# A two-block float32 transformer on one core: PE transposes and squares in the head, the memory's transposes in step 4, and the places of some weight splits

## The reference, cut to what matters

```python
mem_n = rmsnorm(mem, mem_norm)                      # 256 x 1024, used by both layers
for l in range(2):
    x = x + 0.5 * swiglu(rmsnorm(x, g1[l]), gate, up, down)      # 1024 -> 2816 -> 1024
    x = x + mixer(rmsnorm(x, g2[l]))                # l=0: short convolution and window attention; l=1: block attention
    x = x + cross_attention(rmsnorm(x, g3[l]), mem_n, w_q, w_kv, w_o)
    x = x + 0.5 * swiglu(rmsnorm(x, g4[l]), gate, up, down)
x = rmsnorm(x, final_norm)
# second block: swiglu, convolution beside gated linear attention, swiglu, a gated projection, rmsnorm
```

## Time and profile before

| | |
|---|---|
| profiled execution, own time | 1594.08 us |
| its span, first to last instruction | 1592.4 us |
| median of three executions | 1593.88 us |
| PE busy | 98% of the span |
| DVE busy, ACT busy | 71%, 52% |
| mean granted PE clock | 0.996 |

### The profile page before, as it was taken

One profiled execution on the slowest core, in us unless ns is written; L12 is line 12 of the kernel. 1 busy time (PEld: TensorE's weight loads), 2 busy tenths in 40 slices (PEclk: granted clock), 3 DMA queues, 4 the chain that ended last, 5 costly groups with the idle time before them and its releaser, 6 DMA issues.

```text
span 1592.4 us, 23728 instructions
## 1 busy us (share of the span) xinstructions
PE 1563.0 (98%) x9061; PEld 1368.6 (86%) x9061; DVE 1126.9 (71%) x1605; ACT 829.9 (52%) x1164; POOL 80.8 (5%) x139
## 2 busy tenths in 40 slices
PE   8899999999999999999999999999999999999997
PEld 7788899898888888889988888888888998888886
DVE  6776768667666776675766776687666796776666
ACT  5554546555545555455555545455454631554444
POOL 0400002000000000000000190000000000000000
PEclk9999999999999999999999999999999999999999
DMA  8855653545655565555444655546555450456551
GB/s 279 253 176 197 185 184 133 185 133 185 209 187 174 170 212 182 194 182 163 151 133 137 223 196 174 197 150 218 205 184 180 125 185 27 141 210 210 184 187 52
DMA packets 208528, 280.62 MB, mean 176 GB/s; under 512 B 5182, under 2 KB 183784, under 8 KB 208456
## 3 DMA queue, kind: packets, MB, share of 16 engines
q1 hardware_dynamic: 206080, 274.50, 51.6%
q0 software_dynamic: 1360, 3.80, 0.8%
q10 hardware_dynamic: 1016, 1.32, 0.3%
HBM read 278.55 MB, written 2.63 MB: 177 GB/s over the span
## 4 chain that ended last, share of the span: by engine, by line
PE 89%; DVE 7%; ACT 2%; DMA 1%; issue 1%; DVEq 0%; SPq 0%; ACTq 0%
PE bank L1557 38%; PE bank L1608 29%; PE bank L1607 13%; DVE w_lo L946 3%; PE bank L1610 2%; PE bank L2037 2%; PE bank L1666 1%; ACT w_hi L522 1%; PE bank L1815 1%; PE bank L1786 1%; PE bank L1804 1%; DMA raw<-in_ffn_w_up 0%; DMA raw<-in_ffn_w_gate 0%; DMA raw<-in_xa_w_q 0%; ACT xT L550 0%
## 5 line engine op out<-in xcount | busy, mean ns | idle before, releaser
L946 DVE TENSOR_TENSOR w_lo<-raw,w_hi 128x1024 fp32r<-128x1024 f32 x514 | 617.0, 1229 | 221.2 <-ACT w_hi L522 220.4
L1608 PE MATMUL bank<-xT,w_hi 128*128 128x512 f32 x2112 | 734.9, 397 | 1.2 <-DVE w_lo L1217 1.0
L522 ACT ACTIVATE w_hi<-raw 128x1024 fp32r<-128x1024 f32 x514 | 526.4, 1051 | 148.1 <-PE bank L1608 81.7
L1607 PE MATMUL bank<-xT,w_lo 128*128 128x256 f32 x1848 | 516.3, 279 | 0.0
L1608 PEld LDWEIGHTS bank<-xT,w_hi 128*128 128x128 f32 x2112 | 383.0, 188 | 75.9 <-DVE w_lo L1217 1.4
L1607 PEld LDWEIGHTS bank<-xT,w_lo 128*128 128x128 f32 x1848 | 348.9, 189 | 12.1
L1557 PE MATMUL bank<-w_hi,hid_hi 128*128 128x512 f32 x528 | 207.6, 393 | 1.5 <-DVE w_lo L946 1.5
L1557 PE MATMUL bank<-w_hi,hid_lo 128*128 128x512 f32 x528 | 205.8, 390 | 0.0
L1557 PE MATMUL bank<-w_lo,hid_hi 128*128 128x512 f32 x528 | 205.8, 390 | 0.0
L1557 PE MATMUL bank<-xT,w_hi 128*128 128x256 f32 x800 | 146.0, 285 | 1.1 <-DVE w_lo L946 1.1
L1557 PEld LDWEIGHTS bank<-xT,w_hi 128*128 128x128 f32 x800 | 125.2, 192 | 2.5 <-DVE w_lo L946 1.5
(11 more groups left out here) (263 smaller groups left out, 1633.6 us busy)
## 6 DMA issues: line engine op xcount, KB each, us to landing
raw<-in_ffn_w_down SPq DMA_DIRECT2D x44, 1024.0 KB, 5.5
raw<-in_ffn_w_in SPq DMA_DIRECT2D x44, 1024.0 KB, 5.1
raw<-in_ffn_w_gate SPq DMA_DIRECT2D x43, 1024.0 KB, 5.3
raw<-in_ffn_w_up SPq DMA_DIRECT2D x43, 1024.0 KB, 5.4
raw<-in_ffn_w_out SPq DMA_DIRECT2D x22, 1024.0 KB, 5.3
raw<-in_w_in SPq DMA_DIRECT2D x10, 1024.0 KB, 5.3
raw<-in_xa_w_kv SPq DMA_DIRECT2D x8, 1024.0 KB, 5.8
raw<-in_od_w_in SPq DMA_DIRECT2D x8, 1024.0 KB, 5.7
```

What stands on the lines that cost most here:

```text
L522: act.activation(hi, src, ACT.Copy).then_inc(sem["hi_ready"], 1)
L946: dve.tensor_tensor(lo, src, hi.bitcast(F32), ALU.subtract).then_inc(sem["lo_ready"], 1)
L1607: pe.matmul(bank[:, b, T:2 * T], lo, xT_hi[:, k, :], start=False, stop=False)
L1608: last = pe.matmul(bank[:, b, :], hi, xT[:, k, :, :], start=k == 0, stop=k == KD - 1)
```

## The change

1. PE issues 13 transposes of the identity into bank 5 before it waits for the first gains, and 8 more between the transposes of x and the first matmul.
2. In the head ACT does `xT_his` for k 4 to 7 directly behind the splits of halves 0 and 1; the two squares of x stand later, one ahead of and one behind the late splits of halves 2 and 3. DVE's root stands behind those splits.
3. The root of the memory stands between DVE's steps 2 and 3, its scaling is now ACT's, between steps 3 and 4. PE transposes it in the step j=4: banks 0 and 1 between the two down halves (waits for `gate_summed`), banks 2 and 3 behind them (waits for `up_summed`). ACT and DVE take it out behind the hidden values of step 4.
4. At the five borders behind row projections one split stands between the first and the second residual; at the first of them another one moves into `norm`, behind the last residual.
5. In step 0 of every FFN the split base+3 stands ahead of SiLU on ACT, and between the product and `hid_lo` on DVE.

```diff
@@ ACT, ffn_step @@
                     if after_sums is not None:
                         after_sums()
+                    split(i, base + 3)
                     silu()
...
-                for n in range(5 if j == NJ - 1 else 4 if j else 3, n_splits):
+                for n in range(5 if j == NJ - 1 else 4, n_splits):
@@ ACT @@
+            def memory_scale():
+                c.next("mem_rstd_ready")
+                for t in range(NT):
+                    act.activation(mem_in[:, t, :], mem_in[:, t, :], ACT.Copy, scale=mem_rstd[:, t:t + 1])\
+                        .then_inc(sem["mem_normed"], 1)
...
                     ffn_step(f, 2)
-                    ffn_step(f, 3, after_hidden=lambda: xT_his(COL_OF["mem"], memT_hi, by_bank=True))
-                    ffn_step(f, 4)
+                    ffn_step(f, 3)
+                    memory_scale()
+                    ffn_step(f, 4, after_hidden=lambda: xT_his(COL_OF["mem"], memT_hi, by_bank=True))
@@ ACT, head @@
-            act.wait_ge(sem["x_loaded"], 16)
-            act.wait_ge(sem["x1_loaded"], 16)
-            mean_square(0)
-            mean_square(1)
             xT_his(COL_OF["ffn1"], xT_hi, ks=range(4, KD))
             act.wait_ge(sem["second_part_loaded"], 16)
             first_split(2, early, "first_hi_ready")
             first_split(3, early, "first_hi_ready")
+            act.wait_ge(sem["x_loaded"], 16)
+            act.wait_ge(sem["x1_loaded"], 16)
+            mean_square(0)
             act.wait_ge(raw_ready[1], landed[1])
             first_split(2, late, "hi_ready")
             first_split(3, late, "hi_ready")
+            mean_square(1)
@@ DVE, norm and ffn_step @@
                 residual_part(1, 1, scale)
+                splits(n_splits)
                 xT_los(gain, xT_hi, xT_lo, ks=range(4, KD))
...
-                if j == NJ - 1:
-                    split(i, base + 4)
+                if j in (0, NJ - 1):
+                    split(i, base + (4 if j else 3))
                 dve.wait_ge(sem["hidden_hi_ready"], plus(f.j0 + j + 1, 2))
@@ DVE, ffn @@
-                    memory_scale()
                     ffn_step(f, 2)
-                    ffn_step(f, 3, after_hidden=lambda: xT_los(COL_OF["mem"], memT_hi, memT_lo, by_bank=True))
-                    ffn_step(f, 4)
+                    memory_rstd()
+                    ffn_step(f, 3)
+                    ffn_step(f, 4, after_hidden=lambda: xT_los(COL_OF["mem"], memT_hi, memT_lo, by_bank=True))
@@ DVE, head @@
-            rstd_of_both()
             first_split(2, late, "hi_ready", 3, "lo_ready")
             first_split(3, late, "hi_ready", 4, "lo_ready")
+            rstd_of_both()
@@ DVE, borders: ev_w_out, xa_w_o (cross), od_w_out, w_out_2 @@
-            splits(7)
-            add_residual(1.0)
+            splits(5)
+            add_residual(1.0, between=split)
...
-                norm(COL_OF["xa"] + KD * l, scale=1.0, n_done=end, q_factor=128.0 ** -0.5)
+                norm(COL_OF["xa"] + KD * l, scale=1.0, n_done=end, q_factor=128.0 ** -0.5, n_splits=1 - l)
...
-                splits(4)
-                add_residual(1.0)
+                splits(3)
+                add_residual(1.0, between=split)
...
-            splits(8)
-            add_residual(1.0)
+            splits(7)
+            add_residual(1.0, between=split)
...
-            splits(4)
-            add_residual(1.0)
+            splits(3)
+            add_residual(1.0, between=split)
@@ PE, ffn @@
-                        if j == 4 and i is None and n in (0, 2):
+                        if j == 5 and i is None and n in (0, 2):
                             c.next("xT_lo_ready", 2)
...
-                    down(j - 1, v0 + 6 * j + 2, between=memory if j == 3 else None)
+                    if j == 4:
+                        down(j - 1, v0 + 6 * j + 2, between=lambda: memory(0), after=lambda: memory(1))
+                    else:
+                        down(j - 1, v0 + 6 * j + 2)
@@ PE @@
-            def memory():
-
-                c.next("mem_normed", 2)
-                pe.wait_ge(sem["gate_summed"], 4)
-                pe.wait_ge(sem["up_summed"], 4)
-                for k in range(KD):
+            def memory(part):
+
+                if part == 0:
+                    c.next("mem_normed", 2)
+                    pe.wait_ge(sem["gate_summed"], 5)
+                else:
+                    pe.wait_ge(sem["up_summed"], 5)
+                for k in range(4 * part, 4 * part + 4):
...
+            def keep_busy(n):
+
+                for _ in range(n):
+                    pe.transpose(bank[:, 5, 0:P], ident[:, :], ident[:, :])
+
             pe.wait_ge(sem["pool_const"], 4)
+            keep_busy(13)
             pe.wait_ge(sem["first_gains_loaded"], 32)
...
                     x_transposes(t, (k,))
+            keep_busy(8)
             ffn(loaded=True)
```

More of the change, by code:

```diff
@@ L297, in build @@
             hi_ready lo_ready half_done
-            residual mean_sq mem_normed diag_ready scale_psum scale_ready scaled xT_psum xT_hi_ready xT_lo_ready acc_ready
+            residual mean_sq mem_rstd_ready mem_normed diag_ready scale_psum scale_ready scaled xT_psum xT_hi_ready xT_lo_ready acc_ready
             gate_part_ready up_part_ready gate_summed up_summed gate_scaled up_scaled act_gate_ready hidden_ready hidden_hi_ready hidden_lo_ready
@@ L952, in splits, with rsqrt @@
                     split()
-            def rsqrt(dst, src, tmp, tmp2):
+            def rsqrt(dst, src, tmp, tmp2, done="dve_step"):
                 link(dve.tensor_scalar(src, src, EPS, None, ALU.add))
@@ L967, in rsqrt @@
                 link(dve.scalar_tensor_tensor(tmp, tmp, -0.5, src, ALU.mult, ALU.mult))
-                link(dve.scalar_tensor_tensor(dst, tmp, 1.5, dst, ALU.add, ALU.mult))
+                link(dve.scalar_tensor_tensor(dst, tmp, 1.5, dst, ALU.add, ALU.mult), done)
             def rstd_of_both():
@@ L989, in xT_los, with norm @@
                         last.then_inc(sem["xT_lo_ready"], 1)
-            def norm(gain, scale, n_done, q_factor=None):
+            def norm(gain, scale, n_done, q_factor=None, n_splits=0):
                 xT_los(gain, xT_hi, xT_lo, ks=range(4))
@@ L1109, in ffn_step @@
                 else:
-                    for n in range(4 if j else 3, n_splits):
+                    for n in range(4, n_splits):
                         split(i, base + n)
@@ L1196, in y_lo, with memory_rstd @@
                     dve.tensor_tensor(lo, src, hi.bitcast(F32), ALU.subtract).then_inc(sem["y_lo_ready"], 1)
-            def memory_scale():
+            def memory_rstd():
                 c.next("mean_sq", 2)
-                rsqrt(mem_rstd, mem_sq, small[:, 4:6], small[:, 6:8])
-                for t in range(NT):
-                    dve.tensor_scalar(mem_in[:, t, :], mem_in[:, t, :], mem_rstd[:, t:t + 1], None, ALU.mult)\
-                        .then_inc(sem["mem_normed"], 1)
+                rsqrt(mem_rstd, mem_sq, small[:, 4:6], small[:, 6:8], done="mem_rstd_ready")
             def vector_columns():
@@ L1727, in gate_up, with down @@
                         wide(v + n, n, i, between=(lambda: scale_broadcast(4)) if late and j == 1 and n == 2 else None)
-                def down(j, v, i=None, between=None):
+                def down(j, v, i=None, between=None, after=None):
                     ready = j0 + j + 1
@@ L1738, in down @@
                             between()
+                    if after is not None:
+                        after()
                 if loaded:
```

## The result

The changed kernel has a median of 1582.76 us (four executions, 1580.93 to 1585.06); the kernel before, run on the same chip beside it, 1593.11 us (four, 1592.17 to 1595.42). The ratio is 0.9932 with a 95% interval of 0.9919 to 0.9945. The forecast was 1582.7 us. The total came out; the terms that make it did not, as the rest of this document shows. The profiled execution is the longest of the four: 1585.06 us, with a span of 1583.3 us.

The account below looks back on a forecast made before the run. PE, busy for 98% of the span, was taken to bound the kernel. Memory 6.8, borders 2.9, step 0 1.0 and head 0.5 sum to 11.2 us, giving 1582.7 us; own range 1580 to 1584.5, 8 in 10 1579.5 to 1588.5.

Parts of the forecast that it names:

- the memory part: Memory transposes moved to step 4 in halves: 7.1 us of wait and low clock gone, less 0.3 us, worth 6.8 us.
- the head: Start of the kernel, idle transposes and later squares and root: gain 0.5 us, bounds 1.9 us gain to 1.5 us loss.
- the borders: Five borders behind row projections: all PE waits for residuals go, 2.9 us gained, bounds 1.8 to 2.9 us.
- I take 0.3 us: At gate_up(5), behind the memory's second half: PE's new wait would be 0.3 us, near the undisturbed step.
- the upper bound of 2.2 us: At gate_up(5): largest new PE wait, with all 2.1 us of ACT's scalings delaying a step already 1.6 us late.
- loads are issued sooner: First FFN: argument against a moved memory wait, since DVE has lost its scalings; no size of its own.
- the memory's wait moves along: Step 4's up weights reach ACT late, PE waits about 4.2 us at gate_up(5), clock falls: 1589.8 us; chance 0.13.
- PE's next half starts about 0.65 us earlier: End of the head: PE's first half of step 1 starts about 0.65 us sooner; 0.5 us taken on average.
- the forecast's branch: In the head: idle transposes hold PE's clock up; eight transposes behind half 0 take 0.9 us, not 1.63.
- the rival (0.30): In the head: idle transposes do not raise the clock, step 1 starts 1.5 us later, 1584.7 us; chance 0.30.
- The fear of a wait at the residual (1,0): At the borders: the moved remainder (about 1.2 us) delays this residual; gain only 1.8 us if some wait returns.
- Step 0 of the fifth FFN: Split ahead of SiLU lets PE start at 1071.95 instead of 1072.91: 1.0 us gained, bounds 0.5 and 1.3 us.

Follow-up runs that it names:

- the changed kernel's second profile: The changed kernel run once more with nothing changed against it: median 1582.52 us (5 executions).

## Why the prediction was right, and where it was wrong

**The total** (1582.7 forecast, 1582.76 measured) is right by luck, because errors cancel: the memory part was far too large, the head and the borders too small.

**Memory: wrong, in its first sentence.** "Gone are the 4.36 us, 3.65 - 1.75 = 1.90 us of slow transposes and 3.60 - 2.72 = 0.88 us of slow matmuls: 7.1 us" is a correct price of the wait and a wrong assignment. It was priced as if no other part touched that wait. The head's edits already take about 5.5 of the 7.1 us (2.78 us of waiting and 2.78 us of low clock), which left the wait of 1.58 us (with all the other parts 0.71 + 0.68 = 1.4 us). Then "I take 0.3 us" for the new wait failed: it was 1.74 us in one profile and 2.60 us, beyond the upper bound of 2.2 us, in the other. That step assumed that the weights of step 4 come as in an undisturbed step. Its argument "loads are issued sooner" was true (by 5.7 us), but the earlier issue left the load beside POOL's transfers for its whole way, and it landed only 1.2 us sooner. So some 1.5 us of gain and 1.7 us of new wait: nothing.

**The rival "the memory's wait moves along" (0.13)** had half of the mechanism: a late up unit and a wait at `gate_up(5)`, in the profiled execution with a fall of the clock. But the late unit is not the next one, which ACT was to split in step 4: ACT does that split at 86.24 without a wait. It is again the one that ACT got at 72.15 before (70.91 now), and its lag is carried into step 4. The rival had the size wrong (4.2 us), and it, too, counted the old wait as wholly this part's.

**Head: the start of step 1 right, the part wrong.** "PE's next half starts about 0.65 us earlier" is 0.53 to 0.78 us in the profiles. The step that failed is the one that let the head end there. For the borders the text had followed a moved remainder to "SP's load that it releases"; for the two remainders of the head, which free the first `raw` slot, it hadn't. They are what counts: through the late gate unit, 3.0 us for every later load up to the memory.

**Idle transposes: the forecast's branch was right and the rival (0.30) wrong.** Without them the first eight transposes of x take 1.97 us in all five profiled kernels that lack them, and the next eight 1.63 to 1.91 us. With them the first eight take 1.09 to 1.97 us in the nine that have them, and the next eight 1.03 or 1.04 us in every one. In seven of the nine the first eight take under 1.97 us, so the level rose before they were done, with only transposes on PE until then; in the other two it rose within the eight idle ones behind them, which take 1.23 and 1.32 us instead of 1.04. The Trainium skill says that the full clock doesn't engage for transposes (TensorE: Matmul & The Clock Gate, Part 4: PE-mode transpose); these rows contradict it. In time the idle transposes by themselves are worth 1.1 us by the medians, with no change inside the interval.

**Borders: mechanism right, term mis-sized.** All five waits are gone. The sum of 2.9 us took the idle for the cost; it is 4.0 to 4.2 us. Each wait costs about 0.2 us more than its idle, which explains 1.0 us of the difference. The fear of a wait at the residual (1,0) was unfounded.

**Step 0 of the fifth FFN: right.** Forecast 1.0 us, 1.16 us in the chain; the wait that is left was forecast at about 0.5 us and is 0.26.

**The range and the signs.** The median lies in the forecast's own range of 1580 to 1584.5 us; one result can't show how good the chances were. The granted clock was to stay at 1.00 from 20 us on; up to the last 2 us it did in the changed kernel's second profile, and not in the first, so this differs between executions of the same kernel.

## What to carry to other kernels

Price a wait once, and ask of every part of a change whether it reaches that wait: parts that shorten the same one don't add, and the fall of the clock behind it goes to whichever part brings the wait down first. Follow a moved instruction to the load that it releases and to the landing, not only the issue, of every load behind that, since a few microseconds in a prologue can come back where an in-order engine is short of weights much later; and look at what else uses the DMA when the load would now run. At these borders a wait of PE costs its idle plus about 0.2 us of draining and restarting.

## What the runs showed of the hardware

- Transposes of a 128x128 float32 identity on an otherwise unused PE raise its clock to 2.4 GHz: with thirteen idle ones ahead, the next eight take 1.09 to 1.97 us and the eight idle ones behind them 1.03 to 1.32 us (1.04 in seven of nine profiles), where the first eight without them take 1.97 us. The column of the granted clock shows nothing of this; it reads 1.00 through the head of all these kernels, and only the durations tell.
- In the first FFN, PE's clock fell to 1.2 GHz after waits of 2.13, 2.60, 3.07, 3.55, 3.63 and 4.36 us and stayed up after waits of 1.20, 1.36, 1.58 and 1.74 us. It fell during the wait in three of the six and up to 1.4 us behind it in the others; the last is that of 2.13 us, with only transposes on PE between the wait and the fall. One kernel had the 1.74 and the 2.60 us in different executions, so its time steps by the 1.7 us of low clock.
- The same load of 1 MB takes 5.3 to 5.5 us where POOL's transfers are moved away, and 6.8 to 11.7 us beside them (a copy between two places in DRAM, then a load); issued 5.7 us earlier it landed 1.2 us earlier.
